# The experts' first projection in 512-column passes, with GpSimd making the low weights

## The chip, the cores and the metric

One core of one Trainium2 chip runs the whole program. The metric is the time on the device in microseconds (us), the median of three runs. TensorE (PE) multiplies, VectorE (DVE), ScalarE (ACT) and GpSimd (POOL) do the rest, and SyncE (SP) issues the loads of the weights.

## The reference, cut to what matters

The model is a block of two layers (retention, dilated attention, two feed-forward parts), followed by a second block of two layers, each of which mixes tokens and then runs a mixture of 16384 small experts (`peer`). All is float32. Only the experts matter here:

```python
def peer(xn, wq, k1, k2, u_tab, v_tab):
    q = (xt @ wq).reshape(t, PEER_HEADS, D_KEY)        # 256 tokens, 8 heads
    s1 = jnp.einsum("thd,hnd->thn", q1, k1)             # 128 keys a side
    s2 = jnp.einsum("thd,hnd->thn", q2, k2)
    v1, i1 = lax.top_k(s1, TOPK)
    v2, i2 = lax.top_k(s2, TOPK)
    cand = v1[..., :, None] + v2[..., None, :]
    sv, ci = lax.top_k(cand, TOPK)
    experts = e1 * N_KEYS + e2
    gates = jax.nn.softmax(sv, axis=-1)
    ...
        hid = jax.nn.gelu(jnp.einsum("td,tkd->tk", xi, u_tab[ei]))
        return jnp.einsum("tk,tkd->td", gi * hid, v_tab[ei])
```

The kernel gathers no rows. It computes the hidden value of every expert for every token (the first projection, 16384 x 1024 weights), multiplies by a gate that is zero for experts that were not picked, and multiplies by the second table.

## The kernel before, in words

All weights come as a stream of tiles of 128 x 1024 float32, numbered `b`, in four slots. For each, SyncE loads `raw`, ScalarE rounds it into `wh` (helper `hi`, L432), VectorE subtracts to get the rest `wl` (helper `lo`, L942), and TensorE uses both: a product of float32 is made from three float32r products, high x high, high x low and low x high. The activations are split in the same way into `xh` and `xl`, which lie side by side in `xs`, 2 x 256 tokens per block of 128 rows. `hi(b)` needs tile b - 4 to be finished on TensorE (semaphore `mm_done`), `lo(b)` needs `hi(b)`, and TensorE's `wait_tile` needs `lo(b)`.

There are two ways to run a tile of a projection. `tile_a` makes three matmuls of 256 columns for each of the eight blocks of rows (`passes`, L1688 to L1690); the result of 256 tokens lies in one PSUM bank, and ScalarE takes it out. `tile_sums` (L1719 to L1733) makes one matmul of 512 columns (wh against xh and xl at once) and one of 256 (wl against xh); the two halves of the bank then have to be added, which the feed-forward layers have VectorE do (`sum_halves`, L948). Two PSUM banks (`ps_t`) take turns, so a tile must be taken out before the next but one starts (`wait_free`, semaphore `evac`).

In each of the two layers of the second block (k = 0, 1; first tile g0), the experts come in this order: 16 tiles of `peer_wq` with the key scores, then 128 tiles of the first projection (from gu = g0 + 45), then 128 tiles of the second (from gv = g0 + 173). While the first projection runs, VectorE picks the top keys in eight rounds of 47 instructions (L1526 to L1601), with one `lo` after every few of them; the picks end near tile U_PICK = 56. ScalarE goes tile by tile: `hi` of the tile two ahead, then the Gelu of this tile from PSUM into `hid` (helper `run`, L446).

From tile U_FREE = 62 on, 66 tiles are "late": behind each of the first 64 of them stands one step n of the gates, for four tokens. VectorE makes one-hot rows (`onehots`, L1632), ScalarE scales them (`gate_rows`, four of L871), TensorE multiplies them (`gates`, L2248), ScalarE puts the gates of experts whose hidden values are not there yet into `hid` (`put_gates`, L892), and VectorE multiplies the hidden values that are there (`weigh`, L1644). The hidden values of a late tile are split: tokens whose gates are known go to `raw_hid` (L883) and are multiplied by VectorE (`late_weigh`, L1652), the others go straight to `hid` (L885); this is `late_hidden`.

Each engine runs its own program in order. Per late step these are, on VectorE: `lo` of the tile two ahead, `late_weigh(n)`, `weigh(n)` (waits for `put_gates(n)`), `onehots(n+2)`. On ScalarE: `hi` of the tile two ahead, `late_hidden(n)`, `gate_rows(n+1)` (waits for `onehots(n+1)`), `put_gates(n)`. On TensorE: the tile, then `gates(n)`. GpSimd issues some DMAs (gains of the norms, keys) and does no arithmetic.

## Time and profile before

| | us |
|---|---|
| median of three runs | 2810.3 (2809.2 to 2810.81) |
| profiled execution | 2811.18, its span 2809.4 |
| TensorE busy | 2756.2 (98%) |
| VectorE busy | 2004.6 (71%) |
| ScalarE busy | 1568.7 (56%) |
| GpSimd busy | 32.2 (1%), 63 DMA issues |

Busy times of TensorE are pipelined: a matmul's record reaches into the next one's, so the distance between two starts is the pace and the mean duration is not. The late stretch lies from 1254 to 1500 us in the first layer, the search stretch ahead of it from about 1040 us.

### The profile page before, as it was taken

The numbers are of one execution on the slowest core, as the hardware profiler recorded it, in microseconds if no ns is written. First come the engines' busy times: TensorE is split into PE (matmuls) and PEld (weight loads), VectorE is DVE, ScalarE is ACT, GpSimd is POOL, SyncE is SP. The second block draws the span as 40 slices with busy tenths as digits, with TensorE's granted clock in tenths as the row PEclk, the third lists the DMA queues.
The fourth block names the chain that finished last, engine by engine and source line by source line (L and its number), as shares of the span: only waits on it lengthen the run. The fifth ranks groups of instructions, "written<-read, shape, count | busy, mean of one in ns | idle before, by whom it ended". The sixth has DMA issues, their size and how long they took to land.

```text
span 2809.4 us, 49471 instructions
## 1 busy us (share of the span) xinstructions
PE 2756.2 (98%) x17443; PEld 2472.6 (88%) x17443; DVE 2004.6 (71%) x3314; ACT 1568.7 (56%) x2759; POOL 32.2 (1%) x63
## 2 busy tenths in 40 slices
PE   8999999999999999999999999998999999999998
PEld 7888888887887889999998888887999999988887
DVE  6767675676766869977886555577799678855555
ACT  4355454555545665557775555575555677645454
POOL 0000000000000000000000000000000000000000
PEclk9999999999999999999999999999999999999999
DMA  6445656554554345554445555553455444465554
GB/s 214 156 152 181 196 179 203 179 177 143 182 197 156 133 147 176 180 179 141 138 143 173 193 194 193 191 173 114 157 181 185 159 143 137 146 199 193 194 194 165
DMA packets 164944, 480.20 MB, mean 171 GB/s; under 512 B 15840, under 2 KB 58848, under 8 KB 164672
## 3 DMA queue, kind: packets, MB, share of 16 engines
q1 hardware_dynamic: 161424, 467.72, 50.3%
q0 software_dynamic: 3232, 10.20, 1.1%
q8 instruction: 93, 1.52, 0.2%
q14 instruction: 51, 0.42, 0.1%
q10 hardware_dynamic: 144, 0.34, 0.0%
HBM read 477.02 MB, written 1.18 MB: 170 GB/s over the span
## 4 chain that ended last, share of the span: by engine, by line
PE 91%; DVE 5%; ACT 2%; DMA 1%; issue 1%; DVEq 0%; ACTq 0%; POOLq 0%
PE ps L1688 22%; PE ps L1689 22%; PE ps L1690 22%; PE ps L1729 10%; PE ps L1732 5%; PE ps L2248 4%; DVE wl L942 1%; DMA raw<-stream_dram 1%; PE ps L1701 1%; ACT wh L432 1%; DVE arena L1383 1%; DVE xr L962 1%; PE ps L2214 1%; PE ps L1987 0%; PE ps L2030 0%
## 5 line engine op out<-in xcount | busy, mean ns | idle before, releaser
L942 DVE TENSOR_TENSOR wl<-raw,wh 128x1024 fp32r<-128x1024 f32 x878 | 1074.1, 1224 | 569.2 <-ACT wh L432 561.5
L432 ACT ACTIVATE wh<-raw 128x1024 fp32r<-128x1024 f32 x878 | 928.2, 1058 | 493.7 <-DMA raw<-stream_dram 485.1
L1688 PE MATMUL ps<-xs,wh 128*128 128x256 f32 x2576 | 743.7, 289 | 0.3 <-DVE wl L942 0.2
L1689 PE MATMUL ps<-xs,wh 128*128 128x256 f32 x2576 | 729.6, 283 | 0.0
L1690 PE MATMUL ps<-xs,wl 128*128 128x256 f32 x2576 | 729.3, 283 | 0.0
L1688 PE MATMUL ps<-wh,mh 128*128 128x512 f32 x1304 | 509.4, 391 | 2.0 <-DVE wl L942 1.1
L1690 PE MATMUL ps<-wh,ml 128*128 128x512 f32 x1304 | 507.4, 389 | 0.0
L1689 PE MATMUL ps<-wl,mh 128*128 128x512 f32 x1304 | 507.4, 389 | 0.0
L1688 PEld LDWEIGHTS ps<-xs,wh 128*128 128x128 f32 x2576 | 495.0, 192 | 0.8 <-DVE wl L942 0.4
L1689 PEld LDWEIGHTS ps<-xs,wh 128*128 128x128 f32 x2576 | 495.3, 192 | 0.1
L1690 PEld LDWEIGHTS ps<-xs,wl 128*128 128x128 f32 x2576 | 494.5, 192 | 0.0
L1729 PE MATMUL ps<-xs,wh 128*128 128x512 f32 x1344 | 441.4, 400 | 2.1 <-DVE arena L948 1.0
L1732 PEld LDWEIGHTS ps<-xs,wl 128*128 128x128 f32 x1344 | 252.6, 188 | 56.9
L1688 PEld LDWEIGHTS ps<-wh,mh 128*128 128x128 f32 x1304 | 244.8, 188 | 54.9 <-DVE wl L942 4.0
L1690 PEld LDWEIGHTS ps<-wh,ml 128*128 128x128 f32 x1304 | 244.8, 188 | 51.0
L1689 PEld LDWEIGHTS ps<-wl,mh 128*128 128x128 f32 x1304 | 244.8, 188 | 50.5
L1732 PE MATMUL ps<-xs,wl 128*128 128x256 f32 x1344 | 265.2, 278 | 0.0
L1729 PEld LDWEIGHTS ps<-xs,wh 128*128 128x128 f32 x1344 | 210.8, 189 | 10.8 <-issue 7.0
L446 ACT ACTIVATE arena<-ps 128x256 f32 (+1 forms) x188 | 72.0, 384 | 215.1 <-PE ps L1690 214.6
L483 ACT ACTIVATE mh<-arena 128x512 fp32r (+1 forms) x158 | 99.5, 630 | 89.2 <-PE ps L1690 80.2
L954 DVE TENSOR_TENSOR ml<-arena,mh 128x512 fp32r<-128x512 f32 x158 | 108.7, 689 | 46.6 <-ACT mh L483 46.3
L1644 DVE TENSOR_TENSOR arena<-arena,ps 128x252 f32<-128x252 f32 (+42 forms) x128 | 70.2, 549 | 93.4 <-ACT arena L892 93.4
(300 smaller groups left out, 2552.0 us busy)
## 6 DMA issues: line engine op xcount, KB each, us to landing
raw<-stream_dram SPq DMA_DIRECT2D x878, 512.0 KB, 3.3
arena<-norm_rows POOLq DMA_DIRECT2D x32, 128.0 KB, 3.6
picks<-bias_scratch SPq DMA_DIRECT2D x24, 128.0 KB, 3.6
arena<-bias_scratch SPq DMA_DIRECT2D x24, 128.0 KB, 3.6
arena<-keys_dram POOLq DMA_DIRECT2D x16, 128.0 KB, 3.4
arena<-ret_c_dram POOLq DMA_DIRECT2D x1, 1344.0 KB, 5.9
xr<-x_dram POOLq DMA_DIRECT2D x1, 1024.0 KB, 7.9
arena<-rg_w_dram POOLq DMA_DIRECT2D x4, 128.0 KB, 3.2
```

Source lines behind the costliest of these rows:

```text
L432: A(wh[b % 4][:, :, :], raw[:, b % 4, :].rearrange("p (a b) -> p a b", a=DB), ACT.Copy) \
L446: A(dst, src, func, scale=scale, **kw).then_inc(evac, 1)
L483: A(mh[:, s:s + 2, :], src, ACT.Copy).then_inc(m_hi, 1)
L942: V.tensor_tensor(wl[b % 4][:, :, :], raw[:, b % 4, :].rearrange("p (a b) -> p a b", a=DB), wh[b % 4][:, :, :].bitcast(F32), ALU.subtract) ...
L954: V.tensor_tensor(ml[:, s:s + 2, :], src, mh[:, s:s + 2, :].bitcast(F32), ALU.subtract) \
L1644: V.tensor_tensor(h, h, ps_a[:, n % 4, :].rearrange("p (t m) -> p m t", t=4)[:, 0:known, :], ALU.mult).then_inc(g_mul, 1)
L1688: M(out_ap, lh, rh, start=first, stop=False, skip_group_check=skip)
L1689: M(out_ap, lh, rl, start=False, stop=False, skip_group_check=skip)
L1690: return M(out_ap, ll, rh, start=False, stop=last, skip_group_check=skip)
L1729: ins = M(bank, wh[b % 4][:, c, :], xs[:, c, :, :].rearrange("p a t -> p (a t)"), start=(c == 0), stop=(c == DB - 1), skip_group_check=True)
L1732: ins = M(bank[:, 0:T], wl[b % 4][:, c, :], xh[:, c, :], start=False, stop=False, skip_group_check=True)
L2248: ins = M(ps_a[:, n % 4, j * P:(j + 1) * P], gated[n % 3][:, j, :], oh[n % 2][:, 4 + j, :].bitcast(F32), start=True, stop=True)
```

## The change

For 124 tiles of each layer, tiles 4 to 127 of the first projection (248 in all), the change does four things. TensorE runs `tile_sums` in place of `tile_a`. VectorE adds the halves (`hidden_sum`): into `hid`, or for late tiles into `raw_hid`; it takes the place of `lo` in VectorE's program, for the tile three behind in the search stretch. ScalarE's Gelu then works in place on that sum, from SBUF, and waits for the new semaphore `u_sum`. GpSimd makes `wl` of these tiles in a loop of its own after its DMA issues for the keys, and TensorE waits for its semaphore `w_lo_pool`. In the late stretch VectorE's program per step becomes `hidden_sum(n)`, `late_weigh(n)`, `weigh(n)`, `onehots(n+2)`.

```diff
@@ -66,6 +66,19 @@
 START["b0"] = START["ffn1"] + FFN_TILES
 START["b1"] = START["b0"] + B2_TILES
 TILES = START["b1"] + B2_TILES
+U_SUMS, NK_SUMS = 4, NK - 4
+
+
+def is_summed(b):
+    return any(U_SUMS <= b - START[n] - 45 < NK for n in ("b0", "b1"))
+
+
+def low_by_dve(b):
+    return b + 1 - sum(min(max(b + 1 - START[n] - 45 - U_SUMS, 0), NK_SUMS) for n in ("b0", "b1"))
+
+
+def low_by_pool(b):
+    return sum(min(max(b + 1 - START[n] - 45 - U_SUMS, 0), NK_SUMS) for n in ("b0", "b1"))
 
 EV = {"ret": 0, "ffn0": 32, "att": 32 + 4 * FU, "ffn1": 32 + 4 * FU + 48}
 EV["b0"] = EV["ffn1"] + 4 * FU
@@ -222,6 +235,7 @@
 
 
         raw_ready = [sem(f"raw_ready{i}") for i in range(4)]
+        w_lo_pool, u_sum = sem("w_lo_by_gpsimd"), sem("hidden_summed")
         w_hi, w_lo, mm_done, evac = sem("w_hi"), sem("w_lo"), sem("mm_done"), sem("evac")
         m_hi, m_lo = sem("m_hi"), sem("m_lo")
         const_in, vec_in, x_in_s, retc_in, attc_in = sem("const_in"), sem("vectors_in"), sem("x_in"), sem("retc_in"), sem("attc_in")
@@ -407,6 +421,12 @@
                     pool.wait_ge(mm_done, g0 + 30 + 3 * j)
                     for m in range(2):
                         pool.dma_start(pk[:, m, 2 * j:2 * j + 2, :], keys[k, :, m, 2 * j:2 * j + 2, :]).then_inc(k_in[j], 16)
+                with pool.Fori(0, NK_SUMS // 4) as i:
+                    for j in range(4):
+                        b = g0 + 45 + U_SUMS + j
+                        pool.wait_ge(w_hi, i * 4 + b + 1)
+                        nc.gpsimd.tensor_tensor(wl[b % 4][:, :, :], raw[:, b % 4, :].rearrange("p (a b) -> p a b", a=DB),
+                                                wh[b % 4][:, :, :].bitcast(F32), ALU.subtract).then_inc(w_lo_pool, 1)
             pool.wait_ge(m_lo, PAIR["b1"] + 10)
             pool.dma_start(ln_rows[:, 0, :], bass.AP(norm_rows.tensor, V_FIN * P, [[0, P], [1, D]])).then_inc(ln_in, 16)
 
@@ -845,21 +865,31 @@
                     evacuate(gu + q, eu + q, hid[:, q, :], ACT.Gelu_apprx_tanh)
                     if q == 0:
                         keys_scored(3)
-                run(gu + 4, eu + 4, U_PICK - 4, lambda n: one(hid[:, 4:U_PICK, :], n), func=ACT.Gelu_apprx_tanh)
+                def gelu_of_sum(j, i=None, body=0):
+                    act.wait_ge(u_sum, NK_SUMS * k + j - U_SUMS + 1 + (0 if i is None else i * body))
+                    h = hid[:, j, :] if i is None else one(hid[:, U_SUMS:U_PICK, :], i * 4 + j - U_SUMS)
+                    A(h, h, ACT.Gelu_apprx_tanh).then_inc(evac, 1)
+
+                with act.Fori(0, (U_PICK - U_SUMS) // 4) as i:
+
+                    A(unused, ones[:, 0:1], ACT.Gelu_apprx_tanh)
+                    for j in range(4):
+                        hi(gu + U_SUMS + j + 2, i, 4)
+                        gelu_of_sum(U_SUMS + j, i, 4)
                 hi(gu + U_PICK + 2)
-                evacuate(gu + U_PICK, eu + U_PICK, hid[:, U_PICK, :], ACT.Gelu_apprx_tanh)
+                gelu_of_sum(U_PICK)
                 act.wait_ge(pick_step, 8 * PICK_STEPS * (k + 1))
                 A(ge, ge, ACT.Exp).then_inc(p_exp, 1)
                 for j in range(U_PICK + 1, U_PICK + 4):
                     hi(gu + j + 2)
-                    evacuate(gu + j, eu + j, hid[:, j, :], ACT.Gelu_apprx_tanh)
+                    gelu_of_sum(j)
                 act.wait_ge(p_t, k + 1)
                 for c in range(NC_T):
                     A(pickT[:, 0:3, c * P:(c + 1) * P], ps_x[:, c, 0:384].rearrange("p (a b) -> p a b", a=3),
                       ACT.Copy).then_inc(p_tc, 1)
                 for j in range(U_PICK + 4, U_FREE):
                     hi(gu + j + 2)
-                    evacuate(gu + j, eu + j, hid[:, j, :], ACT.Gelu_apprx_tanh)
+                    gelu_of_sum(j)
 
                 def gate_rows(n):
 
@@ -875,14 +905,12 @@
                 def late_hidden(n):
 
                     g, m, known = gu + U_FREE + n, U_FREE + n, min(4 * n, T)
-                    act.wait_ge(mm_done, g + 1)
-                    src = ps_t[:, (eu + m) % 2, 0:T]
-                    if n:
-                        if n >= 3:
-                            act.wait_ge(g_late, (U_LATE - 1) * k + n - 2)
-                        ins = A(raw_hid[n % 2][:, 0:known], src[:, 0:known], ACT.Gelu_apprx_tanh)
+                    act.wait_ge(u_sum, NK_SUMS * k + m - U_SUMS + 1)
+                    src = raw_hid[n % 2]
                     if known < T:
                         ins = A(hid[:, m, known:T], src[:, known:T], ACT.Gelu_apprx_tanh)
+                    if n:
+                        ins = A(raw_hid[n % 2][:, 0:known], src[:, 0:known], ACT.Gelu_apprx_tanh)
                     ins.then_inc(evac, 1)
 
                 def put_gates(n):
@@ -1493,6 +1521,18 @@
 
 
                 gu = g0 + 45
+
+                def hidden_sum(j, dst):
+                    dve.wait_ge(mm_done, gu + j + 1)
+                    V.tensor_reduce(dst, ps_t[:, (e0 + 33 + j) % 2, :].rearrange("p (a t) -> p t a", a=2), AX, ALU.add) \
+                        .then_inc(u_sum, 1)
+
+                def lo_or_sum(b):
+                    if not is_summed(b):
+                        lo(b)
+                    elif is_summed(b - 3):
+                        hidden_sum(b - 3 - gu, hid[:, b - 3 - gu, :])
+
                 at = [0]
                 for q in range(6):
                     lo(g0 + 29 + q + 2)
@@ -1519,7 +1559,7 @@
 
                     def tile():
                         so_far(i)
-                        lo(g0 + 29 + at[0] + 2)
+                        lo_or_sum(g0 + 29 + at[0] + 2)
                         at[0] += 1
 
                     def key_at(a, s, half, of):
@@ -1612,15 +1652,15 @@
                     assert pick[0] == PICK_STEPS
                 assert at[0] <= 16 + U_PICK
                 for j in range(at[0] - 16 + 2, U_PICK + 4):
-                    lo(gu + j)
+                    lo_or_sum(gu + j)
 
                 dve.wait_ge(p_exp, k + 1)
                 link(V.tensor_reduce(gd[:, 0, :], ge, AX, ALU.add))
                 link(V.reciprocal(gd[:, 1, :], gd[:, 0, :]))
                 V.tensor_tensor(ge, ge, gd[:, 1, :].unsqueeze(2).to_broadcast([P, NC_T * H2, 16]), ALU.mult) \
                     .then_inc(p_e, 1)
-                for j in range(U_PICK + 4, U_FREE + 2):
-                    lo(gu + j)
+                for j in range(U_PICK + 4, U_FREE + 3):
+                    lo_or_sum(gu + j)
 
                 dve.wait_ge(p_tc, 2 * (k + 1))
 
@@ -1655,7 +1695,9 @@
                 onehots(1)
                 gv, u0 = g0 + 173, PAIR[f"b{k}"]
                 for n in range(U_LATE):
-                    lo(gu + U_FREE + n + 2)
+                    if not is_summed(gu + U_FREE + n + 2):
+                        lo(gu + U_FREE + n + 2)
+                    hidden_sum(U_FREE + n, raw_hid[n % 2])
                     if n:
                         late_weigh(n)
                     if n < U_STEPS:
@@ -1690,7 +1732,10 @@
                 return M(out_ap, ll, rh, start=False, stop=last, skip_group_check=skip)
 
             def wait_tile(b, i, body):
-                pe.wait_ge(w_lo, b + 1 + (0 if i is None else i * body))
+                if is_summed(b):
+                    pe.wait_ge(w_lo_pool, low_by_pool(b) + (0 if i is None else i * body))
+                else:
+                    pe.wait_ge(w_lo, low_by_dve(b) + (0 if i is None else i * body))
 
             def wait_free(e, i, ebody):
                 if e >= 2:
@@ -2223,9 +2268,9 @@
                     tile_a(g0 + 45 + q, e0 + 33 + q)
                     if q == 0:
                         key_scores(3)
-                run(tile_a, g0 + 49, e0 + 37, U_PICK - 4)
+                run(tile_sums, g0 + 49, e0 + 37, U_PICK - 4)
                 for j in range(U_PICK, U_PICK + 4):
-                    tile_a(g0 + 45 + j, e0 + 33 + j)
+                    tile_sums(g0 + 45 + j, e0 + 33 + j)
 
                 pe.wait_ge(p_e, k + 1)
                 for c in range(NC_T):
@@ -2234,7 +2279,7 @@
                                                   src[:, 8 * c:8 * c + 8, :].rearrange("p h j -> p (h j)"), ident)
                 ins.then_inc(p_t, 1)
                 for j in range(U_PICK + 4, U_FREE):
-                    tile_a(g0 + 45 + j, e0 + 33 + j)
+                    tile_sums(g0 + 45 + j, e0 + 33 + j)
 
                 def gates(n):
 
@@ -2250,7 +2295,7 @@
                     ins.then_inc(g_mm, 1)
 
                 for n in range(U_LATE):
-                    tile_a(g0 + 45 + U_FREE + n, e0 + 33 + U_FREE + n)
+                    tile_sums(g0 + 45 + U_FREE + n, e0 + 33 + U_FREE + n)
                     if n < U_STEPS:
                         gates(n)
                 pe.wait_ge(g_mul, U_STEPS * (k + 1))
```

## Rows read from the trace of the kernel before

**Rows 1.** The page: span, and busy us (share, instructions) of each engine.

```profile
span 2809.4 us, 49471 instructions
PE 2756.2 (98%) x17443; PEld 2472.6 (88%) x17443; DVE 2004.6 (71%) x3314; ACT 1568.7 (56%) x2759; POOL 32.2 (1%) x63
```

**Rows 2.** Table by stage: stretch, length, busy us (instructions) by engine, clock, DMA share, GB/s.

```profile
1120.00:1190.00 70.00, 70.00 (x586) 70.00 (x585) 67.93 (x221) 35.36 (x54) 0.00 (x0) 1.00 0.55 184
...
1260.00:1470.00 210.00, 210.00 (x1790) 210.00 (x1789) 167.20 (x225) 153.08 (x448) 0.00 (x0) 1.00 0.42 141
```

**Rows 3.** TensorE's timeline, search stretch: start us, us, engine, line, operation; 72 matmuls apart.

```profile
1149.75 0.28 PE L1688 MATMUL ps<-xs,wh 128*128 128x256 f32 x1
...
1158.39 0.28 PE L1688 MATMUL ps<-xs,wh 128*128 128x256 f32 x1
```

**Rows 4.** TensorE's timeline, a tile_sums of the feed-forward layer: six blocks apart.

```profile
300.01 0.40 PE L1732 MATMUL ps<-xs,wl 128*128 128x256 f32 x2
...
302.10 0.39 PE L1732 MATMUL ps<-xs,wl 128*128 128x256 f32 x2
```

**Rows 5.** ScalarE's timeline, late stretch: put_gates of steps 0 and 62.

```profile
1258.42 0.37 ACT L892 ACTIVATE arena<-ps 128x260 f32<-128x260 f32 x1
...
1491.42 0.17 ACT L892 ACTIVATE arena<-ps 128x12 f32<-128x12 f32 x1
```

**Rows 6.** VectorE's timeline, one late step (in brackets: idle before, releaser).

```profile
1341.88 1.22 DVE L1632 TENSOR_TENSOR mh<-cst,pickT 128x1024 fp32r<-128x1024 f32 x1
1343.01 1.22 DVE L942 TENSOR_TENSOR wl<-raw,wh 128x1024 fp32r<-128x1024 f32 x1
1344.15 0.25 DVE L1652 TENSOR_TENSOR arena<-arena,picks 128x92 f32<-128x92 f32 x1
1345.21 0.51 DVE L1644 TENSOR_TENSOR arena<-arena,ps 128x344 f32<-128x344 f32 x1 [0.81 <-ACT arena L892]
1345.64 1.22 DVE L1632 TENSOR_TENSOR ml<-cst,pickT 128x1024 fp32r<-128x1024 f32 x1
```

**Rows 7.** ScalarE's timeline, the same late step.

```profile
1343.28 0.25 ACT L883 ACTIVATE picks<-ps 128x92 f32<-128x92 f32 x1 [1.00 <-PE ps L1690]
...
1343.61 1.27 ACT L871 ACTIVATE picks<-mh,pickT 128x128 f32<-128x128 f32 x4
1344.78 0.30 ACT L892 ACTIVATE arena<-ps 128x168 f32<-128x168 f32 x1
1344.97 1.06 ACT L432 ACTIVATE wh<-raw 128x1024 fp32r<-128x1024 f32 x1
```

**Rows 8.** Timelines of VectorE and ScalarE, feed-forward layer: a sum, and the activation behind it.

```profile
364.12 0.68 DVE L948 TENSOR_REDUCE arena<-ps 128x256 f32<-128x512 f32 x1
...
364.83 0.42 ACT L462 ACTIVATE arena<-arena 128x256 f32<-128x256 f32 x1 [1.89 <-DVE arena L948]
365.16 1.04 ACT L432 ACTIVATE wh<-raw 128x1024 fp32r<-128x1024 f32 x1
```

**Rows 9.** VectorE's timeline, search stretch: parts of one round, eight tiles long.

```profile
1094.21 1.23 DVE L942 TENSOR_TENSOR wl<-raw,wh 128x1024 fp32r<-128x1024 f32 x1
...
1107.66 0.68 DVE L1529 TENSOR_TENSOR mh<-picks,cst 128x512 fp32r<-128x512 f32 x1
...
1110.35 0.19 DVE L1601 TENSOR_TENSOR picks<-picks 128x32 f32<-128x32 f32 x1
...
1111.17 1.23 DVE L942 TENSOR_TENSOR wl<-raw,wh 128x1024 fp32r<-128x1024 f32 x1
...
1114.47 1.23 DVE L942 TENSOR_TENSOR wl<-raw,wh 128x1024 fp32r<-128x1024 f32 x1
...
1117.44 1.23 DVE L942 TENSOR_TENSOR wl<-raw,wh 128x1024 fp32r<-128x1024 f32 x1
```

**Rows 10.** Table by stage (columns as in rows 2), around a norm between two blocks.

```profile
880.00:890.00 10.00, 9.27 (x40) 7.12 (x40) 7.23 (x10) 5.79 (x7) 0.00 (x0) 1.00 0.30 103
890.00:900.00 10.00, 4.07 (x19) 3.61 (x18) 8.03 (x16) 6.29 (x14) 0.00 (x0) 0.73 0.50 159
```

## The prediction, made before the changed kernel was run

> **What bounds the kernel now.** I read the page first: TensorE is busy for 2756.2 of 2809.4 us [rows 1]. That is an average, and a busy TensorE can still be paced by someone else, so the next view is the table by stage for the two stretches that the change touches [rows 2]. In the search stretch (tiles of the experts' first projection up to U_PICK, while VectorE picks the top keys) VectorE is busy 67.93 of 70 us. In the late stretch (the 66 tiles from U_FREE on, with one step of gates behind each of 64) VectorE has 80% and ScalarE 73%. TensorE is busy all the time in both, so the timelines must tell how much slack the others have.
>
> TensorE's pace: the matmuls of a `tile_a` start 0.120 us apart (72 of them from 1149.75 to 1158.39) [rows 3], so a tile takes 24 x 0.120 = 2.88 us. The same work as `tile_sums` can be seen in the feed-forward layers: two blocks of 128 rows take (302.10 - 300.01) / 3 = 0.697 us [rows 4], so a tile's eight blocks take 2.79 us. The busy means of single matmuls (283 and 400 ns) would mislead here: they overlap; the distance of starts is the pace.
>
> The late stretch's pace: `put_gates` starts at 1258.42 for n = 0 and at 1491.42 for n = 62 [rows 5], 233.0 / 62 = 3.758 us a step: a tile (2.88) and the four gate matmuls (the other 0.88). In this step VectorE goes through L1632 `onehots`, L942 `lo`, L1652 `late_weigh`, then stands still until ScalarE's L892, then L1644 `weigh` [rows 6]; ScalarE goes through L883 and L885 `late_hidden`, four of L871 `gate_rows`, L892 `put_gates`, L432 `hi`, and then waits some 1.0 us for TensorE [rows 7]. The reader should see that ScalarE and VectorE already hand work to each other once a step, with the slack of about a microsecond.
>
> **The change part by part.**
> *TensorE.* 248 tiles go from 2.88 to 2.79 us: 0.09 us each. Of these 116 lie before the late stretch (58 in each of two layers): at most 116 x 0.09 = 10.4 us. In the late stretch a step of TensorE would be 2.79 + 0.88 = 3.67 us.
>
> *The late stretch, where the change costs.* Before, `late_hidden(n)` on ScalarE needs only TensorE's tile. Now it needs VectorE's `hidden_sum(n)`, and that stands in VectorE's program behind `onehots(n+1)`. This closes a loop through two engines that are each in order: onehots(n+2), hidden_sum(n+1) on VectorE; late_hidden(n+1), gate_rows(n+2), put_gates(n+1) on ScalarE; weigh(n+1), onehots(n+3) on VectorE. Each piece waits for the one ahead, by the program's order or by a semaphore, and one turn is one step. Before, `lo` stood at the place of the sum and waited for nothing in the loop, and ScalarE started gate_rows without waiting for VectorE's newest work. The turn, by starts:
> onehots to the next VectorE instruction, 1343.01 - 1341.88 = 1.13 us [rows 6];
> the sum of 2 x 256 columns from PSUM, 0.68, and 0.03 until ScalarE starts on it [rows 8] (the same instruction in the feed-forward layer);
> late_hidden: from PSUM its two pieces took 1343.61 - 1343.28 = 0.33 [rows 7]. Now they read SBUF. A piece of 256 columns from SBUF holds ScalarE for 365.16 - 364.83 = 0.33 by itself [rows 8], and there are two pieces that share 256 columns: between 0.33 and 0.66, and nearer to the lower end since the columns are divided; I take 0.45;
> gate_rows to put_gates 1344.78 - 1343.61 = 1.17, put_gates 0.30 [rows 7];
> its end (1345.08) to weigh 0.13, weigh to onehots 1345.64 - 1345.21 = 0.43 [rows 6] (as n grows put_gates shrinks and weigh grows by as much).
> Sum: 1.13 + 0.68 + 0.03 + 0.45 + 1.17 + 0.30 + 0.13 + 0.43 = **4.32 us a step**, bounds 4.20 and 4.53, against 3.67 that TensorE needs and 3.758 now. Over 62 steps and two layers: 124 x (4.32 - 3.758) = +70 us (+55 to +96). The ends: the first put_gates comes about 1 us later (two onehots now stand behind the last early sum), while the last steps, without onehots, are shorter and TensorE has run ahead; I put them at nothing, within 3 us a layer.
> What else is queued there: `late_weigh` (0.25 us) runs beside gate_rows, and `hi` (1.06) beside weigh, onehots and the sum; both stay covered. TensorE waits for put_gates and gate_rows, and the output tile's next user waits for the Gelu rather than for TensorE's own pace, so TensorE idles about 0.65 us a step.
>
> *The search stretch.* VectorE's eight tiles with one round of picks take 1117.44 - 1094.21 = 23.23 us, against 8 x 2.88 = 23.04 of TensorE: VectorE is just about the bound already [rows 9]. Eight `lo` at 1.14 by starts (1344.15 - 1343.01 [rows 6]) leave 14.1 us of picks; eight sums of 0.66 to 0.68 give 19.5, against 8 x 2.79 = 22.3 of TensorE. So the sums fit, the longest part too (3.30 - 1.14 + 0.68 = 2.84 us, one tile's time, once a round). The sum's way to TensorE, 0.68 + 0.03 + a Gelu of 0.4, must be done within one tile's time, since two PSUM tiles take turns: 1.6 us are left for VectorE to be late.
>
> *GpSimd.* It does no arithmetic in this trace; its 63 instructions [rows 1] are DMA issues, and all of them stand ahead of this loop in each layer or behind it. Its price for the subtraction is not seen. The nearest row is VectorE's own, 1.22 us; an engine that takes in the two operands one after the other would need twice that, 2.45. Both are under TensorE's 2.79, so the engine keeps up; I take the upper end. ScalarE's `hi` stands behind the Gelu of the tile three ahead, so it is done 0.71 + 0.4 + 1.06 = 2.2 us after that tile, and two tiles' time, 5.6 us, less this leaves 3.4 us for GpSimd. Hence low weights are no bound on the sum, by a small margin. What this engine does to VectorE beside it no row shows. The bounds for the search stretch: TensorE's full gain, -10 us, or, where GpSimd and VectorE hinder each other, +20 us (worked out under the rivals). I take +5, the middle, since no row is nearer to one end.
> The Trainium skill, "GPSIMD Engine Reference", section 3.1, measures a two-input elementwise operation at 1.96 times VectorE's time; that would be 2.40 us here, an estimate, and changes nothing.
>
> Sum: 2811.2 (the profiled execution, 0.9 above the median of 2810.3; span 2809.4) + 70 + 5 = **2886 us**.
>
> **The rivals.**
> *GpSimd and VectorE can't read at the same time.* Against the forecast of an undisturbed VectorE: its instructions with two SBUF operands and GpSimd's subtraction would exclude each other. In a round, the last three tiles hold four such instructions on 512 columns (two L1529, two L1533; 0.68 each by L1529) and three small ones (0.19 by L1601) [rows 9]: 3.3 us, with 3 x 2.45 of GpSimd 10.7 us against 8.4 of TensorE: 2.3 lost, 0.7 gained by the round's faster matmuls, 13 rounds in the changed tiles (52 tiles a layer): +20 us. In the late stretch onehots 1.22 + 2.45 + late_weigh 0.25 + weigh 0.43 and three handoffs of 0.03 make 4.44, hardly more than the loop: +15. Time: 2811 + 70 + 20 + 15 = 2916. Nothing in the trace speaks for or against, as GpSimd computes nothing there. The Trainium skill, "SBUF — State Buffer", section "Who interferes with whom", says just this: a VectorE instruction with two SBUF inputs contends with a GpSimd instruction that reads SBUF, and the second to come waits for the whole of the first. No run here shows it yet. 25%.
> *GpSimd slower than a tile.* It decides from 2.79 us on. At 3.1 us and without mutual waits the 116 early tiles cost 0.22 each over now: 2811 + 70 + 26 = 2907; with mutual waits the late step becomes 1.22 + 3.1 + 0.25 + 0.43 + 0.1 = 5.1, 95 us more, some 3000. 8%.
> *Faster: the loop has slack that I don't see.* If VectorE's sum is out before onehots or the turn is under 3.67 us, TensorE sets the pace everywhere: 2811 - 248 x 0.09 = 2789. For it: VectorE stands 0.8 us a step today, and the sum is 0.5 us shorter than the subtraction. Against it: that idle time is the wait for put_gates, which is a link of the loop; the sum and late_hidden would have to lose 0.65 of their 1.16 us, and the program's order leaves no other place for them. 6%.
> *TensorE's clock falls in the late stretch.* With a step at half speed (7.3 us) the time would go beyond 3200. Against it: where TensorE lacked 0.73 us of 10 the granted clock stayed at 1.00 (2.4 GHz); it fell to 0.73, part of the time 1.2 GHz, behind an idle stretch of 5.9 us [rows 10]. 2%.
>
> **How the numbers follow.** Forecast 57%, 2850 (both lower bounds, and the ends 6 shorter) to 2915; mutual waits 25%, up to 2950; slow GpSimd 8%, 2907 to 3000; faster 6%; clock 2%; and 2% for a turn so near 3.76 that nothing is seen. The range 2850 to 2950 leaves out the faster cases and most of the last ones. Faster by over 0.2% (about what a measurement of this kernel can tell from no change) 6%, within it 2%, slower 92%.
>
> **What would show it.** Right: in the late stretch put_gates 4.2 to 4.5 us apart; ScalarE waiting ahead of late_hidden for VectorE's sum, not for TensorE; VectorE waiting for put_gates still; TensorE idle some 0.65 us a step at full clock; the search stretch within 2% of now. Wrong: put_gates 3.7 apart (the loop has slack); onehots or L1533 stretched, or idle ahead of them, beside GpSimd's subtraction (mutual waits); TensorE waiting for `w_lo_by_gpsimd` (GpSimd slow); L1644 idle behind late_weigh rather than put_gates.

## The result, and the profile after

The changed kernel takes 2954.7 us (median of 4 runs, 2953.8 to 2956.5) against 2810.6 for the kernel before (4 runs): 1.0516 times as long (95% interval 1.0503 to 1.0528). The direction was forecast and the time was not: 2886 us was said, and 2954.7 lies 5 us beyond the upper end of the range, 2950. The profiled execution took 2953.8, its span is 2952.0, which is 142.6 us more than before's 2809.4.

The head of the page of the changed kernel (busy us, share of the span and count by engine), and its line for the new GpSimd work (busy us, mean ns | idle before):

```profile
PE 2797.5 (95%) x15459; PEld 2375.8 (80%) x15459; DVE 2106.1 (71%) x3314; ACT 1572.5 (53%) x2759; POOL 712.9 (24%) x311
...
L428 POOL TENSOR_TENSOR wl<-raw,wh 128x1024 fp32r<-128x1024 f32 x248 | 680.6, 2746 | 343.8 <-ACT wh L452 341.4
```

They answer to [rows 1]. VectorE gave up 248 subtractions of 1.22 us for as many sums of 0.69, 131 us less by that, and yet is busy 100 us longer than before. Something stretched what was left on it. That is the thread to pull.

The table by stage (columns as in [rows 2]) for the search stretch, the late stretch, and ten microseconds in which the search stretch begins:

```profile
1081.00:1300.00 219.00, 187.26 (x1009) 158.00 (x1008) 181.06 (x474) 91.35 (x148) 147.25 (x61) 0.95 0.46 149
1310.00:1580.00 270.00, 248.11 (x1496) 208.59 (x1496) 220.43 (x252) 173.88 (x492) 185.59 (x61) 1.00 0.38 124
1090.00:1100.00 10.00, 6.38 (x25) 5.20 (x24) 8.74 (x31) 2.73 (x4) 3.94 (x3) 0.70 0.33 105
```

TensorE was never without work in either stretch before [rows 2]; now it lacks work in both.

**Where the 142.6 us are.** The marks of [rows 5], the first `put_gates` of a layer, tell the two stretches apart. In the first layer it starts 41.8 us later than before (1300.22 against 1258.42), and from there to the last one, 63 spacings on, it takes 268.8 us against 236.2, another 32.6. In the second layer the two parts are 35.0 (from the first layer's last `put_gates` to the second layer's first) and 32.6. What is behind the last is 0.6: 41.8 + 32.6 + 35.0 + 32.6 + 0.6 = 142.6. So the late stretch took 65 of them, about what was forecast for it, and the search stretch 77 (with what the end of the first layer gives back), where 5 had been said.

**The search stretch.** ScalarE's timeline (start us, us, engine, line, operation, in brackets the idle time before and who ended it), three of the eight Gelus of a round, and the first of the next round:

```profile
1110.27 0.42 ACT L871 ACTIVATE arena<-arena  x1 [1.41 <-DVE arena L1527]
...
1115.84 0.42 ACT L871 ACTIVATE arena<-arena  x1 [4.20 <-DVE arena L1527]
...
1124.62 0.42 ACT L871 ACTIVATE arena<-arena  x1 [4.98 <-DVE arena L1527]
...
1138.86 0.42 ACT L871 ACTIVATE arena<-arena  x1 [1.42 <-DVE arena L1527]
```

From 1110.27 the eight distances are 5.57, 2.25, 6.53, 2.43, 3.44 and three times 2.79: 28.59 us a round, where TensorE needs 8 x 2.79 = 22.3 and the kernel before took 23.0. Three tiles run at TensorE's pace, two catch up a little, one is 0.7 us late, and two come 2.8 and 3.7 us late. Those two times ScalarE waited for VectorE's sum. What held VectorE stands in its timeline, beside GpSimd's for the same time:

```profile
1108.93 2.40 POOL L428 TENSOR_TENSOR wl<-raw,wh 128x1024 fp32r<-128x1024 f32 x1 [0.18 <-ACT wh L452]
1111.72 2.40 POOL L428 TENSOR_TENSOR wl<-raw,wh 128x1024 fp32r<-128x1024 f32 x1 [0.38 <-ACT wh L452]
1117.28 5.21 POOL L428 TENSOR_TENSOR wl<-raw,wh 128x1024 fp32r<-128x1024 f32 x2 [3.17 <-ACT wh L452]
```

```profile
1110.05 1.33 DVE L1624 TENSOR_SCALAR picks<-picks 128x32 uint32<-128x32 uint32 x1
...
1111.74 2.43 DVE L1630 SCALAR_TENSOR_TENSOR picks<-picks 128x32 f32<-128x32 f32 x1
...
1115.01 0.69 DVE L1527 TENSOR_REDUCE arena<-ps 128x256 f32<-128x512 f32 x1
...
1117.26 0.69 DVE L1527 TENSOR_REDUCE arena<-ps 128x256 f32<-128x512 f32 x1
1117.87 2.36 DVE L1569 TENSOR_TENSOR ml<-picks,cst 128x512 fp32r<-128x512 f32 x1
1120.26 2.77 DVE L1573 TENSOR_TENSOR ml<-ml,picks 128x512 fp32r<-128x512 f32 x1
...
1123.79 0.69 DVE L1527 TENSOR_REDUCE arena<-ps 128x256 f32<-128x512 f32 x1
```

L1624 and L1630 work on 32 columns. The first starts while GpSimd works from 1108.93 to 1111.33, and ends at 1111.38; the second starts 0.02 us behind the subtraction of 1111.72 to 1114.12, and ends at 1114.17. L1569 starts in the first of the pair of 1117.28, which is over at 1117.28 + 2.40 = 1119.68, and ends 0.55 later, about its own length; L1573 comes just behind the start of the pair's second, which ends at 1122.49, and ends 0.54 behind it. So each ends close behind GpSimd, as if it had waited until GpSimd was done. The sums (L1527, out of PSUM) keep their 0.69, but those of 1115.01 and 1123.79 stand behind these waits.

The groups by line for VectorE, 1090 to 1255 us (busy us, mean ns | idle before), first before, then after; the lines differ by 40 (L1533 is now L1573, L1590 is L1630):

```profile
L1533 DVE TENSOR_TENSOR ml<-ml,picks 128x512 fp32r<-128x512 f32 x7 | 4.8, 692 | 0.2
...
L1529 DVE TENSOR_TENSOR ml<-picks,cst 128x512 fp32r<-128x512 f32 x6 | 4.1, 685 | 0.0
...
L1590 DVE SCALAR_TENSOR_TENSOR picks<-picks 128x32 f32<-128x32 f32 x6 | 1.2, 192 | 0.2
...
L1584 DVE TENSOR_SCALAR picks<-picks 128x32 uint32<-128x32 uint32 x6 | 1.0, 174 | 0.0
```

```profile
L1527 DVE TENSOR_REDUCE arena<-ps 128x256 f32<-128x512 f32 x46 | 31.8, 691 | 13.1 <-PE ps L1774 12.2
L1573 DVE TENSOR_TENSOR ml<-ml,picks 128x512 fp32r<-128x512 f32 x6 | 14.6, 2428 | 0.2
L1630 DVE SCALAR_TENSOR_TENSOR picks<-picks 128x32 f32<-128x32 f32 x6 | 14.4, 2402 | 0.2
L1569 DVE TENSOR_TENSOR ml<-picks,cst 128x512 fp32r<-128x512 f32 x6 | 12.5, 2081 | 0.1
L1624 DVE TENSOR_SCALAR picks<-picks 128x32 uint32<-128x32 uint32 x6 | 6.8, 1138 | 0.0
```

The last four stand in a round once each. They alone make 1.74 + 2.21 + 1.40 + 0.96 = 6.3 us a round. In the steady rounds (1095 to 1238 us), with the smaller ones, all groups but subtractions and sums (each mean times its number in a round) go from 15.9 to 23.5, +7.6. With 14.1 us of picks, as the prediction had them, and 8 x 0.69 of sums, VectorE needs 19.6 + 7.6 = 27.2 us a round, 4.9 more than TensorE. The rest of the 28.6 is VectorE idle, waiting for TensorE (13.1 us in 165, some 2.3 a round, of which some 0.8 are in the 14.1 already, from 5.0 us in 143 before): the lateness comes in two bursts, and with two PSUM tiles neither engine can work far ahead of the other. Five such rounds, 1110.27 to 1252.01, are 26.5 of the 41.8 us; the six tiles ahead of them, where GpSimd's loop starts, lose another 6.6, and the last tiles up to `put_gates` the rest.

**The late stretch.** One step after, by VectorE, ScalarE and GpSimd in turn; it answers to [rows 6, 7]:

```profile
1382.48 1.22 DVE L1672 TENSOR_TENSOR ml<-cst,pickT 128x1024 fp32r<-128x1024 f32 x1
1383.61 0.68 DVE L1527 TENSOR_REDUCE picks<-ps 128x256 f32<-128x512 f32 x1
1384.87 1.18 DVE L1692 TENSOR_TENSOR arena<-arena,picks 128x80 f32<-128x80 f32 x1 [0.58 <-ACT picks L913]
1386.35 0.50 DVE L1684 TENSOR_TENSOR arena<-arena,ps 128x332 f32<-128x332 f32 x1 [0.29 <-ACT arena L920]
1386.76 1.22 DVE L1672 TENSOR_TENSOR mh<-cst,pickT 128x1024 fp32r<-128x1024 f32 x1
```

```profile
1384.33 0.35 ACT L911 ACTIVATE arena<-picks 128x176 f32<-128x176 f32 x1 [1.45 <-DVE picks L1527]
...
1384.74 1.27 ACT L901 ACTIVATE picks<-ml,pickT 128x128 f32<-128x128 f32 x4
1385.92 0.30 ACT L920 ACTIVATE arena<-ps 128x180 f32<-128x180 f32 x1
```

```profile
1382.96 3.00 POOL L428 TENSOR_TENSOR wl<-raw,wh 128x1024 fp32r<-128x1024 f32 x1 [1.30 <-ACT wh L452]
```

The loop is the one that was described: onehots at 1382.48, sum 1383.61, `late_hidden` 1384.33, `gate_rows` 1384.74, `put_gates` 1385.92, `weigh` 1386.35, the next onehots 1386.76, which is 4.28 us. Over 62 spacings the mean is (1566.99 - 1300.22) / 62 = 4.303. ScalarE waits for the sum (1.45), VectorE waits for `put_gates` (0.29). GpSimd is seen here too: `late_weigh` (L1692) takes 1.18 us instead of 0.25 and ends at 1386.05, 0.3 before `weigh` could start. It is hidden, barely.

### The profile page after: what moved, and what is told of

Its sections match the earlier page's. It is cut to its first block, busy times and chain, and to the rows that moved or that the text cites. A ratio compares the mean times of both kernels' runs of the same rounds, so it can differ in the third digit from the quotient of the medians.

```text
span 2952.0 us, 46057 instructions
## 1 busy us (share of the span) xinstructions
PE 2797.5 (95%) x15459; PEld 2375.8 (80%) x15459; DVE 2106.1 (71%) x3314; ACT 1572.5 (53%) x2759; POOL 712.9 (24%) x311
## 3 DMA queue, kind: packets, MB, share of 16 engines
HBM read 477.02 MB, written 1.18 MB: 162 GB/s over the span
## 4 chain that ended last, share of the span: by engine, by line
PE 57%; DVE 15%; issue 12%; POOL 7%; ACT 7%; DMA 1%; DVEq 0%; POOLq 0%; ACTq 0%
PE ps L1730 13%; PE ps L1731 12%; PE ps L1732 12%; PE ps L1774 10%; POOL wl L428 7%; PE ps L1777 5%; ACT picks L901 4%; DVE mh L1672 3%; DVE picks L1527 3%; DVE ml L1672 2%; DVE arena L1692 2%; DVE wl L970 1%; ACT picks L913 1%; PE ps L1746 1%; ACT wh L452 1%
## 5 line engine op out<-in xcount | busy, mean ns | idle before, releaser
L1774 PE MATMUL ps<-xs,wh 128*128 128x512 f32 x3328 | 1119.0, 405 | 59.8 <-ACT arena L871 47.2
L970 DVE TENSOR_TENSOR wl<-raw,wh 128x1024 fp32r<-128x1024 f32 x630 | 770.6, 1224 | 540.1 <-ACT wh L452 536.8
L428 POOL TENSOR_TENSOR wl<-raw,wh 128x1024 fp32r<-128x1024 f32 x248 | 680.6, 2746 | 343.8 <-ACT wh L452 341.4
L1777 PEld LDWEIGHTS ps<-xs,wl 128*128 128x128 f32 x3328 | 632.2, 190 | 139.3
L1777 PE MATMUL ps<-xs,wl 128*128 128x256 f32 x3328 | 661.8, 280 | 0.0
L1774 PEld LDWEIGHTS ps<-xs,wh 128*128 128x128 f32 x3328 | 532.5, 191 | 83.6 <-ACT arena L871 55.2
L1692 DVE TENSOR_TENSOR arena<-arena,picks 128x256 f32<-128x256 f32 (+42 forms) x130 | 157.4, 1210 | 74.7 <-ACT picks L913 74.7
L871 ACT ACTIVATE arena<-arena (+1 forms) x116 | 48.4, 417 | 235.1 <-DVE arena L1527 235.1
L1730 PE MATMUL ps<-xs,wh 128*128 128x256 f32 x592 | 172.3, 291 | 0.4 <-DVE wl L970 0.2
L1732 PE MATMUL ps<-xs,wl 128*128 128x256 f32 x592 | 169.1, 286 | 0.0
L1731 PE MATMUL ps<-xs,wh 128*128 128x256 f32 x592 | 169.1, 286 | 0.0
L911 ACT ACTIVATE arena<-picks 128x256 f32<-128x256 f32 (+42 forms) x128 | 40.0, 313 | 187.6 <-DVE picks L1527 187.6
L982 DVE TENSOR_TENSOR ml<-arena,mh 128x512 fp32r<-128x512 f32 x158 | 108.7, 688 | 41.5 <-ACT mh L503 41.0
```

Source lines behind the costliest of these rows:

```text
L428: nc.gpsimd.tensor_tensor(wl[b % 4][:, :, :], raw[:, b % 4, :].rearrange("p (a b) -> p a b", a=DB), wh[b % 4][:, :, :].bitcast(F32), ALU.s ...
L970: V.tensor_tensor(wl[b % 4][:, :, :], raw[:, b % 4, :].rearrange("p (a b) -> p a b", a=DB), wh[b % 4][:, :, :].bitcast(F32), ALU.subtract) ...
L982: V.tensor_tensor(ml[:, s:s + 2, :], src, mh[:, s:s + 2, :].bitcast(F32), ALU.subtract) \
L1692: V.tensor_tensor(h, h, raw_hid[n % 2][:, 0:min(4 * n, T)], ALU.mult).then_inc(g_late, 1)
L1730: M(out_ap, lh, rh, start=first, stop=False, skip_group_check=skip)
L1731: M(out_ap, lh, rl, start=False, stop=False, skip_group_check=skip)
```

## The experiments

Two theories stood against each other. **The loop alone:** the step of the late stretch is the turn of the loop, and the search stretch is late for some reason that lies in the sums. **GpSimd's reads:** a VectorE instruction with both operands in SBUF waits for the whole of a GpSimd instruction that reads SBUF, in VectorE's order, and the sums behind it wait as well. A third, that GpSimd's time per tile is what costs, is tested by the kernels that cut its instructions up. The eight kernels differ in who reads what and when.

Kernels come to the search stretch up to 4 us earlier or later than before does, from differences further ahead. So its cost is counted in the first layer from one and the same point ahead of it to the first `put_gates`: the point is where ScalarE takes the `peer_wq` tile out that follows the third pair of key scores, 4.66 us behind the one ahead of it (at 1067.17 before, 1067.20 after). All costs are against before, in us; each ratio is against runs of the kernel before that were taken beside it:

| kernel | sums on VectorE | GpSimd | ScalarE's order | search, 1st layer | late, 1st layer, 63 spacings | median, us (ratio) |
|---|---|---|---|---|---|---|
| before | no | nothing | as before | 0 | 0 | 2810.6 |
| after | yes | 1 subtraction | as before | +41.8 | +32.6 | 2954.7 (1.0516) |
| e1_swap | yes | 1 subtraction | swapped | +41.5 | +29.8 | 2948.3 (1.0489) |
| e2_writes_only | yes | 1 memset | as before | -4.0 | +32.5 | 2865.8 (1.0190) |
| e5_swap_writes | yes | 1 memset | swapped | -4.0 | -2.8 | 2793.6 (0.9939) |
| e6_split2 | yes | 2 halves | as before | +28.0 | +32.9 | 2930.3 (1.0419) |
| e3_split4 | yes | 4 quarters | as before | +16.9 | +32.9 | 2911.4 (1.0351) |
| e8_swap_split4 | yes | 4 quarters | swapped | +16.6 | +4.6 | 2852.7 (1.0147) |
| e4_pool_only | no | 1 subtraction | as before | +7.2 | +41.0 | 2902.7 (1.0326) |
| e7_pool_only_split4 | no | 4 quarters | as before | +11.4 | +3.5 | 2836.6 (1.0090) |

**e2_writes_only: GpSimd writes zeros as low weights and reads nothing.** Its loop is written out in this kernel, with the same waits.

```diff
-nc.gpsimd.tensor_tensor(wl[b % 4][:, :, :], raw[:, b % 4, :]..., wh[b % 4][:, :, :].bitcast(F32), ALU.subtract)
+nc.gpsimd.memset(wl[b % 4][:, :, :].bitcast(F32), 0.0)
```

> GpSimd writes zeros in place of the low weights of the 248 tiles (the product low x high is left out) and so reads nothing from SBUF; all waits and all other work are the same. The theory of mutual waits (in the search stretch VectorE's instructions with two SBUF operands, and its copies, stand still behind GpSimd's subtraction, and the sums stand behind them): L1630's 2.4 us go back to 0.19 and L1573's 2.8 to 0.69, a round of picks takes 22.3 us (TensorE's time) instead of 28.6; the late step stays at 4.2 to 4.3, since the loop sets it. Time 2955 - 2 x 44 = 2867. Rival (the sums by themselves make VectorE or the path over PSUM too slow in the search stretch): round still 28, time about 2950.

Measured: 2865.8 us, 1.0190 times before (1.0173 to 1.0207). The search stretch's cost is gone; even the gain of the faster matmuls shows (-4.0 us). VectorE's groups, 1090 to 1255 us, are those of before:

```profile
L1572 DVE TENSOR_TENSOR ml<-ml,picks 128x512 fp32r<-128x512 f32 x7 | 4.8, 691 | 0.2
...
L1629 DVE SCALAR_TENSOR_TENSOR picks<-picks 128x32 f32<-128x32 f32 x6 | 1.2, 193 | 0.2
```

The late stretch's cost stays, 4.27 to 4.32 us a step. So the two stretches have two causes: GpSimd's subtractions make the search stretch's cost, and the loop makes the late stretch's, with no help of GpSimd.

That it is their reads, and not only their length, these groups don't show: a memset takes 0.95 us in place of 2.40, and of the four stretched instructions only the one-operand L1623 (L1624 in after) starts in one, once in these 165 us. It has to be read where the two meet (VectorE, then GpSimd): here in the second layer,

```profile
2460.74 1.22 DVE L1671 TENSOR_TENSOR mh<-cst,pickT 128x1024 fp32r<-128x1024 f32 x1
```

```profile
2460.71 0.95 POOL L428 MEMSET wl<- 128x1024 f32 x1 [3.35 <-ACT wh L451]
```

and here in the first, just ahead of these 165 us:

```profile
1086.10 0.72 DVE L1623 TENSOR_SCALAR picks<-picks 128x32 uint32<-128x32 uint32 x1
```

```profile
1085.83 0.95 POOL L428 MEMSET wl<- 128x1024 f32 x1 [26.66 <-ACT wh L451]
```

These onehots start 0.03 us behind a memset and keep their 1.22 us; behind a subtraction they take 3.38 (e1, below). The memsets that start while onehots run keep their 0.95, where a subtraction takes 3.00. So it is the reads that hold an instruction with two operands, on the evidence of these few meetings. The one-operand L1623 waits for the memset as well: it ends at 1086.82, the memset at 1086.78.

**e1_swap: take `late_hidden` out of the way of `gate_rows` on ScalarE.** If the turn of the loop sets the step, work that needn't be in it can be moved behind.

```diff
-                    late_hidden(n)
                     if n + 1 < U_STEPS:
                         gate_rows(n + 1)
+                    late_hidden(n)
```

> ScalarE's order in a late step changes: gate_rows(n+1) goes ahead of late_hidden(n), so that it runs beside VectorE's sum. The loop theory (the late step of 4.28 us is one turn through onehots, sum, late_hidden, gate_rows, put_gates, weigh): the sum leaves the turn, 1.22 + 0.03 + 1.17 + 0.42 + 0.30 + 0.13 + 0.43 = 3.7 us; if GpSimd's subtraction of 2.4 us also has to fit between onehots and late_weigh without overlap, the step stops at about 3.9. Time 2955 - 124 x 0.38 = 2908 with exclusion, 2955 - 124 x 0.58 = 2883 without it. The rival theory (the late step is set by GpSimd's own time or by TensorE's waits for the low weights): step still 4.28, time 2955.

Measured: 2948.3 us (1.0471 to 1.0506), 6 us less than after, where 47 had been expected with exclusion. Behind the first step (3.81) they are 3.75 us apart, as they should be without the sum in the loop, and around n = 22 the expected 3.91; but they grow to 4.08, and from n = 44 on every other step takes 6.3 us. VectorE's and GpSimd's timelines there:

```profile
1502.72 3.38 DVE L1672 TENSOR_TENSOR mh<-cst,pickT 128x1024 fp32r<-128x1024 f32 x1
```

```profile
1502.62 2.39 POOL L428 TENSOR_TENSOR wl<-raw,wh 128x1024 fp32r<-128x1024 f32 x1 [0.58 <-ACT wh L452]
```

`weigh` grows with n, so onehots come later, until GpSimd is ahead of them: at n = 43 onehots start first, at 1468.28 against 1468.29, and at the next step GpSimd does, at 1472.36 against 1472.38. From then on onehots wait for all of it in every other step (3.38 instead of 1.22 us above). The step is a race between two engines, and a few hundredths of a microsecond decide over 2.2. This had not been priced: the expectation took the wait of one step for that of all.

**e5_swap_writes: both edits.**

> Both edits of e1 and e2: gate_rows ahead of late_hidden, and GpSimd writes zeros in place of the low weights (the product low x high of the 248 tiles is left out), so nothing contends with VectorE. The loop theory: the late step is 3.70 to 3.76 us from the first step to the last, with neither e1's growth to 4.08 nor its alternation of 6.3 and 3.8; search stretch as in e2. Time 2866 - 2 x 35 = 2796. If something other than the sum's place in the turn held the late step at 4.28: 2866. If e1's growth came from longer weigh and not from GpSimd: some 2815.

Measured: 2793.6 us, 0.9939 times before (0.9923 to 0.9956). The first 40 steps or so are 3.66 to 3.71 us (3.67 was TensorE's sum in the prediction), but for one of 4.05; then they grow to 3.87 at the end, where `late_weigh`, grown from 0.20 us at n = 10 to 0.41, waits for `late_hidden` and holds up `weigh`. With the loop cut and the subtractions gone most of TensorE's own gain is there, 16 us of 248 x 0.09 = 22. The low weights are zeros here, so a product is left out; what it shows is that the two causes account for nearly all of the change's cost.

**e4_pool_only: the other half of the change.** The kernel before, with GpSimd making the low weights of the same tiles, and no sums on VectorE.

```diff
+                with pool.Fori(0, NK_SUMS // 4) as i:
+                    ...
+                        nc.gpsimd.tensor_tensor(wl[b % 4]..., raw..., wh..., ALU.subtract).then_inc(w_lo_pool, 1)
-                if i is None and b >= TILES:
+                if i is None and (b >= TILES or is_summed(b)):
                     return
...
```

> The kernel before, but GpSimd makes the low weights of the 248 tiles: no sums, 256-column passes, ScalarE takes the tiles out of PSUM itself. Theory: VectorE still waits behind GpSimd in the picks (14.1 + 7.5 = 21.6 us a round), but nothing that TensorE needs stands behind these, so the search stretch costs nothing (round 23.0 of TensorE). In the late stretch onehots 1.22, GpSimd 2.4, late_weigh 0.25 and weigh 0.43 exclude one another in a ring, 4.2 us a step against 3.76: time 2811 + 124 x 0.43 = 2864. Without exclusion: 2811. If GpSimd's time per tile (2.4 to 3.0) were what costs, the search stretch would lose too: over 2870.

Measured: 2902.7 us (1.0309 to 1.0343), 39 more than expected. In the search stretch VectorE's instructions are stretched as much as in after (L1549 2195 ns, L1553 1901, L1617 1932 in the same stretch; by the same sum a round's groups take 27.2 us, +11.3), and its rounds are 25.9 us long (L1610 starts at 1159.71 and at 1185.64), longer than TensorE's 23.0. But it costs only 7.2 us in the layer: with neither subtractions nor sums VectorE has nothing that TensorE waits for until the picks are done. Before, ScalarE came for them 9.9 us after they were done (1230.62, 1240.56); here they are done 14.9 us later, counted from the same point, and ScalarE waits for them once, 5.0 us. **A wait costs what stands behind it.** The late stretch shows the race again, from n = 15 on, as steps of 6.0 and 3.3 us by turns (VectorE, then GpSimd):

```profile
1400.12 1.22 DVE L1652 TENSOR_TENSOR mh<-cst,pickT 128x1024 fp32r<-128x1024 f32 x1
1401.25 2.51 DVE L1672 TENSOR_TENSOR arena<-arena,picks 128x132 f32<-128x132 f32 x1
...
1404.15 3.17 DVE L1652 TENSOR_TENSOR ml<-cst,pickT 128x1024 fp32r<-128x1024 f32 x1
```

```profile
1400.54 3.07 POOL L428 TENSOR_TENSOR wl<-raw,wh 128x1024 fp32r<-128x1024 f32 x1 [3.58 <-ACT wh L452]
1403.84 2.40 POOL L428 TENSOR_TENSOR wl<-raw,wh 128x1024 fp32r<-128x1024 f32 x1 [0.23 <-ACT wh L452]
```

Where onehots are first (1400.12), GpSimd waits for them: its 3.07 us hold 0.67 of waiting. Where GpSimd is first (1403.84 against 1404.15), onehots wait. In after this doesn't happen, since the slower loop keeps GpSimd's start behind that of onehots.

**e3_split4 and e6_split2: shorter GpSimd instructions.** If VectorE waits for whole instructions, shorter ones should cost less.

```diff
+                        for q in range(4):                       # e6_split2: 2
+                            s = slice(q * DB // 4, (q + 1) * DB // 4)
-                        nc.gpsimd.tensor_tensor(wl[b % 4][:, :, :], ...)
+                            ins = nc.gpsimd.tensor_tensor(wl[b % 4][:, s, :], ...)
```

> GpSimd's subtraction of a tile is cut into four instructions of 128x256, with the semaphore on the last. Mutual waits that last as long as one GpSimd instruction: VectorE waits at most 0.65 us at a time instead of 2.4; 6 waits a round of at most 0.6 make a round of 22.3 to 24 us; time 2955 - 2 x 30 to 2 x 42 = 2871 to 2895. If GpSimd's throughput were the cause, four instructions in place of one would make it slower: 2955 to 3000. If the two share the port bit by bit, not instruction by instruction, nothing changes: 2955.

> GpSimd's subtraction in two instructions of 128x512. From the measured 2.37 us for 1024 columns and 0.72 for 256, one of 512 should take 1.27, a tile 2.55: under TensorE's 2.79, where four pieces (2.88) are over it. If a wait lasts as long as one GpSimd instruction, the 6.9 us of waits in a round fall to about half, VectorE's round to 23 against 22.3 of TensorE; loss in the search stretch 5 to 15 us a layer in place of 42. Time 2880 to 2900, 2890. If the length of the hold didn't matter: 2955; if only GpSimd's throughput mattered: slower than 2955.

Measured: 2911.4 us (1.0333 to 1.0368) with quarters, 2930.3 (1.0402 to 1.0437) with halves. Both are faster than after and both slower than expected; the late stretch is untouched (+32.9). A tile costs GpSimd more in pieces (2.88 us in quarters against 2.40) and the kernel is faster, so it isn't GpSimd's time per tile that costs in after. For halves, VectorE's groups in the search stretch tell why:

```profile
L1577 DVE TENSOR_TENSOR ml<-ml,picks 128x512 fp32r<-128x512 f32 x7 | 10.6, 1509 | 0.2
...
L1631 DVE CAST picks<-picks 128x96 f32<-128x96 uint32 x6 | 7.7, 1280 | 0.2
L1602 DVE TENSOR_TENSOR picks<-picks 128x96 f32<-128x96 f32 x6 | 7.6, 1273 | 0.2
L1604 DVE TENSOR_TENSOR picks<-picks 128x104 f32<-128x104 f32 x6 | 7.0, 1172 | 0.0
```

A wait is half as long, and more instructions meet one: L1631, L1602 and L1604, that took 0.21 and 0.26 us before, now wait a microsecond each. By the sum of all groups a round has +7.4 us of waits, hardly less than the +7.6 of whole subtractions; only the bursts are smaller. With quarters it is +4.4, and another bound comes in:

```profile
L430 POOL TENSOR_TENSOR wl<-raw,wh 128x256 fp32r<-128x256 f32 x992 | 818.1, 857 | 169.1 <-ACT wh L456 167.9
```

```profile
PE ps L1778 <- POOL wl L430: 12.7, 18, 1.7
```

(The second is the waits view, 1081 to 1280 us: total, times, longest.) A quarter takes 0.72 us alone, a tile's four 2.88 and more, and TensorE needs 2.79: it waits 12.7 us for GpSimd in that stretch. The rival "GpSimd slower than a tile" is thus seen, in the kernel where the split made it so.

**e7_pool_only_split4 and e8_swap_split4: quarters, with the loop absent or cut.**

> e4 with the subtraction in four instructions of 128x256. Hold by instruction: in the late stretch VectorE waits at most 0.72 us at a time, the alternation of 6.0 and 3.3 goes, the step is 3.76 to 3.9; in the search stretch GpSimd's four pieces (2.88 us and waits) are as long as a tile of TensorE (2.88), a few us lost. Time 2815 to 2835, 2822. If the alternation had another cause than the length of the hold: 2903.

> The changed kernel with both mends: gate_rows ahead of late_hidden, GpSimd in four pieces. Search stretch as in e3 (18 us a layer lost, GpSimd's throughput), late step 3.75 to 3.9 in place of 4.28 to 4.32, and no alternation since VectorE's onehots wait at most 0.72 us. Time 2911 - 124 x 0.47 = 2853. If e1's alternation returns with short pieces: 2900.

Measured: 2836.6 us (1.0073 to 1.0107) without sums, just above the range expected; 2852.7 (1.0130 to 1.0164) with sums and the swap, where 2853 was expected. In both, the steps by turns are gone from the late stretch: 3.76 to 3.94 and 3.76 to 3.98 us, but for a few single steps. What is left of their costs is GpSimd's own pace (28.6 us of TensorE's waiting for L430 in e8's whole run) and the search stretch; without sums, quarters cost it more than whole subtractions did (11.4 against 7.2), with GpSimd busy for 179.0 of the 181 us from 1081 to 1262. Of the kernels that compute everything, none is faster than the kernel before.

## Why the prediction was right and wrong

*The late stretch: right, in mechanism and size.* 4.32 us a step was worked out, 4.303 measured; +70 for 124 spacings, 2 x 33.8 = 67.5 by the same spacings. The pieces hold as well: `late_hidden` 1384.74 - 1384.33 = 0.41 (0.45 was taken between 0.33 and 0.66), `gate_rows` 1.18 (1.17), sum to `late_hidden` 0.72 (0.71). e2 gives the same steps without GpSimd's subtractions, and e5 gives 3.66 to 3.71 for most steps when the loop is cut, so the loop is shown to be the cause. The ends, put at nothing, gave back 1.1 us a layer at the last step.

*TensorE's pace: right.* A tile takes 2.79 us where nothing else holds it, as in three distances of the round above, and the gain of 0.09 us for 58 tiles a layer, 5.2, less the microsecond by which the prediction had the first `put_gates` later, comes near the -4.0 of e2 and e5.

*GpSimd's pace: right.* 2.40 us alone (2.45 was taken, from twice VectorE's 1.22), under TensorE's 2.79. Where a subtraction shows 3.00 or 3.07, VectorE was in it first.

*The search stretch: wrong, and this is the step that failed.* It was put at +5, "the middle, since no row is nearer to one end", between -10 and +20. It is +77 for the two layers together. The upper bound was the mistake, and it has three parts that the runs show.
First, the rival summed up the time for which the two engines need the same thing (3.3 us of VectorE and 7.4 of GpSimd, 10.7 in all, against 8.4 of TensorE) and lost only the excess, 2.3 us a round. But VectorE works in order and waits with its hands empty: L1630 needs 0.19 us and took 2.43. The price of one meeting is what is left of GpSimd's instruction, not VectorE's short need. Four instructions alone lost 6.3 us a round.
Second, it counted only instructions with two SBUF operands in the last three tiles. L1624 (one operand, from 0.17 us to a mean of 1.14) waits too, and in e6 a CAST does.
Third, it spread the loss over the round. The prediction itself had the number that decides: 1.6 us for which VectorE can be late with a sum before TensorE waits. L1624 and L1630 in a row are 3.4 us late, L1569 and L1573 3.8; both bursts go beyond it, once each a round, and TensorE can't make that up.
Why waits no shorter cost e4 just 7 us says it from the other side. VectorE's slack was 23.0 - 14.1 = 8.9 us a round there, and the waits (+11.3) used up more than that; but only the end of the picks was late, by 14.9 us, and 9.9 of these were covered. With the sums on VectorE the slack is 22.3 - 19.6 = 2.7 us a round, and every late sum holds TensorE. Sums without subtractions cost nothing in this stretch (e2, -4.0), GpSimd alone little (e4, +7.2), and both together +41.8: costs of two edits don't add up where each takes the other's cover.

*The rival "can't read at the same time": its mechanism is the one that is there.* It had 25%, and 2916. In the late stretch it put +15, and there it cost nothing in after: GpSimd's start is set by `hi`, which stands behind `put_gates` on ScalarE, and `late_weigh` takes the wait beside `gate_rows` with 0.3 us to spare. e1 and e4 show what it costs there as soon as the loop is faster: up to 2.3 us every other step.
The Trainium skill, "SBUF — State Buffer", section "Who interferes with whom", says that whoever starts first, a VectorE instruction with two SBUF inputs or a GpSimd instruction that reads SBUF, holds the shared ports for its whole instruction, and that a GpSimd instruction that only writes is no hindrance to it. This case's trace agrees: L1630 ends at 1114.17, with GpSimd's subtraction (1114.12), onehots that start in one of e2's memsets keep their 1.22 us, and there are waits on either side (3.00 us for GpSimd's 2.40). The page was given 25% where the nearest row said nothing at all; a rule stated so plainly, about just the two operations that the change sets side by side, was worth more than the absence of a row.

*The clock.* It was right for the late stretch: a step is 0.63 us longer than TensorE's 3.67 (its timeline shows 0.34 of them as idle), and the granted clock is 1.00 (2.4 GHz). It fell in the search stretch, which had not been thought of: 0.95 over 219 us, and 0.70, part of the time 1.2 GHz, in the ten microseconds that hold TensorE's first and longest wait, 3.6 us. From 1200 to 1210 us, with TensorE busy for 6.24 of 10, it was 1.00. At most 219 x 0.05 = 11 us of the first layer's loss are the lower level of 1.2 GHz, an estimate from the row of 219 us; how much of this fell into time in which TensorE had nothing to do anyway is open. Of the rest, the waits view of 1081 to 1300 us has 30.2 us of TensorE's own:

```profile
PE ps L1774 <- ACT arena L871: 25.1, 13, 3.6
...
PE ps L1774 <- POOL wl L428: 5.1, 10, 0.8
```

*The signs that were named* told the causes at once: `put_gates` within the 4.2 to 4.5 us, ScalarE's wait ahead of `late_hidden`, and, for mutual waits, L1533 (now L1573) stretched beside GpSimd. The sign that failed was the search stretch within 2% of before.

## What to carry to other kernels

Before work goes to GpSimd, list what VectorE does beside it with operands in SBUF, and charge each such instruction that meets one the rest of a whole GpSimd instruction; then look at what stands behind it in VectorE's order and by how much that may be late. An engine that gains slack from one edit and waits from another must be costed with both in place: where nothing stood behind these waits until the picks' end they cost 7 us in the first layer, and with TensorE's sums behind them 42. And a loop through two engines in order can be priced by adding the distances of starts along it; here that was right within half a per cent.

## What had not been expected of the hardware

- Halving GpSimd's instructions hardly reduced VectorE's waits (+7.4 us a round against +7.6), as more of VectorE's instructions met one. A quarter-size subtraction took 0.72 us, a half 1.27 and a whole one 2.40, so four quarters are 2.88.
- A start a few hundredths of a microsecond earlier or later decides which of two engines waits for the other (e1: onehots 1.22 or 3.38 us), and the step then goes by turns: 6.3 and 3.7 to 3.9 us in e1, 6.0 and 3.3 in e4.
- Short one-operand instructions on VectorE waited as well (L1624, 174 to 1138 ns; a CAST in e6, 210 to 1280), while the sums out of PSUM kept their 691 ns beside GpSimd.
- GpSimd's memset of 128x1024 took 955 ns and did not hold onehots, which have two operands (1.22 us, started 0.03 us behind it); a one-operand instruction of 32 columns (L1623 in e2) that started in a memset waited for it (0.72 us; L1584 before, 0.17).
